# Sample-attention tail of a decoder layer: block choice moved ahead of the value compression

## The chip, the cores and the metric

The kernel runs as one program on one core of a Trainium2 chip (trn2). The metric is the device time of one execution in microseconds (us), the median of several runs. [...]

## What is computed

One decoder layer serves a prompt of 512 rows and 8 sample rows with the same weights. After the input projection, each sample row attends in three ways (native sparse attention) and to a memory; the outputs are normed, projected, and followed by a mixture of 32 experts. The part that the change touches is the attention of the 8 sample rows, over caches of 1024 past rows:

```python
def compress_blocks(rows, pe, w1, w2):      # blocks of 32 rows, every 16 rows
    ...
    return jax.nn.gelu(flat @ w1) @ w2      # once for keys (kc), once for values (vc)

def nsa_core(q, q_pos, gates, kc, vc, kc_end, ks_blk, vs_blk, kw, vw, kw_pos):
    ...
    p_c = masked_softmax(s_c, ...)          # s_c = q . kc, compressed branch
    o_c = p_c @ vc
    imp = sum of p_c over the heads of a group, then over the 4 compressed blocks of a selected block
    top_s, idx = lax.top_k(imp + forced, 16)    # block choice
    o_s = masked_softmax(q . k_sel) @ v_sel     # selected branch
    o_w = masked_softmax(q . kw) @ vw           # window branch
    return gates[..., 0:1] * o_c + gates[..., 1:2] * o_s + gates[..., 2:3] * o_w
```

So the compressed keys are needed for the block choice, and the compressed values only for `o_c`. With 16 of 17 blocks chosen, the choice is one block of the past to leave out.

## The kernel before

The program is written by engine: for each stage, a function for TensorE (`tensor`), VectorE (`vector`), ScalarE (`scalar`), GpSimd (`gpsimd`) and the DMA queue of SyncE (`sync`) writes that engine's instructions in the order in which they will run. Semaphores tie them together: an engine stops at a `wait_ge`, and all that is behind it in its list stops with it. `Chain.then` (L172) counts VectorE's steps in the semaphore `steps_d`; `marks[...]` are counts at named steps on which other engines wait.

`project_and_stream` (L1028) runs two stages as one block: `project` and `stream`. `stream` (L494) reads the caches sequence by sequence, turns them (transposes on TensorE), and forms the scores of the 8 sample rows as each sequence passes. Compression goes in three groups of three sequences, `j` = 0, 1, 2. For a group, `compress(j, q, taps)` (L880) accumulates 16 taps (matmuls of 128x378) for keys (`q` = 0) or values (`q` = 1) in PSUM bank 6 or 7; `gelu(j, q)` (L586) is five VectorE steps with one ScalarE `tanh` (L810) between the fourth and the fifth; `blocks_k` (L921) and `blocks_v` (L928) apply the second weight; `keep_k` and `keep_v` (L600, L604) copy the result to SBUF.

The change lies in the tail of `stream`, after the last sequence, where only group 2 is left. The order of each engine's list there is:

- TensorE (L958 to L1022): the key taps of group 2; the last sequence's scores; ten value taps; `blocks_k(2)`; six value taps; the compressed scores (L966, "cs"); `blocks_v(2)`; the sum of importances (L971, waits for the mark `pc`); the transposes of memory, window and compressed probabilities (L975 to L980, wait for `wp` and `cg`); a matmul with zeros that clears the output bank (L985); a wait for the turned probabilities in SBUF (`pT_ready` 1); a second clearing matmul (L992); value products of the window branch (L994, L997), of the compressed branch (L999) and of the memory (L1002); the transposes of the selected probabilities (L1005, L1006, wait for `sp`); a wait (`pT_ready` 2); value products of the selected branch (L1009, L1012); a wait (`oT_ready`); the gathering of all outputs into one row per sequence (L1021).
- VectorE (L656 to L713): `gelu(2, 0)`; peaks of the memory scores and window scores; `keep_k(2)`; `gelu(2, 1)`; `keep_v(2)`; softmax weights of memory and window (mark `wp`); the peak of the compressed scores (mark `cmax`), their weights (`pc`), their gate (`cg`); the block choice (L684 to L693); the peak of the selected scores (`smax`); four copies of turned probabilities from PSUM (L697 to L700); weights of the selected branch (`sp`); two copies (L706, L707); copies of the outputs (L709, L710) and of the gathered rows (L712, L713).
- ScalarE (L826 to L840): `tanh(2, 0)`, the exponentials of memory, window, `tanh(2, 1)`, the exponentials of the compressed and the selected scores.

GpSimd and SyncE have finished their lists of this stage by then. The block ends with a barrier of all engines (L1058, `close`, L194), and all that follows (`attend` for the prompt, the output projection, the experts with their weight streaming) is issued behind it; the first instruction behind it on SyncE is L1194.

## Time and profile before

| | us |
|---|---|
| median of 3 runs | 1080.23 (1079.83 to 1081.94) |
| span of the profiled execution, first to last instruction | 1077.6 |
| lies around the span, by the median | 2.6 |
| tail of `stream`: first value tap of group 2 to the end of the last copy | 289.89 to 333.92 |
| first DMA issue behind the barrier | 335.05 |

The profile gives no other time of the profiled execution than its span; the 2.6 us are the difference to the median of the runs. Over the whole span TensorE is busy 85%, VectorE 30%, ScalarE 18%, GpSimd 10%. Times in the rows below are us from the start of the span, durations us unless marked ns. One float32 matmul shows as two records, so "x20" are ten taps.

### The profile page before, as it was taken

To read this page: it belongs to the slowest core of one execution; us is meant where nothing else is said; L and a number is where in the kernel's file an instruction comes from. 1 tells how busy PE (TensorE), PEld (TensorE's weight loads), DVE (VectorE), ACT (ScalarE), POOL (GpSimd) and SP (SyncE) were. 2 spreads that over 40 slices of the span, in tenths; PEclk is the share of its full clock that TensorE was granted. 3 is DMA by queue.
4 is the path that set the end of the run, shared out by engine and by line. 5 is a ranking of instruction groups with operands and counts; after the bars stand their busy time and mean duration, and the time that the engine had idled before them with its cause. 6 is when DMAs were issued, how large, how long until landed. Compare 5 with 4: busy or idle time off the path is not lost.

```text
span 1077.6 us, 13517 instructions
## 1 busy us (share of the span) xinstructions
PE 913.1 (85%) x5419; PEld 496.5 (46%) x5419; DVE 324.4 (30%) x697; ACT 193.2 (18%) x462; POOL 112.9 (10%) x131
## 2 busy tenths in 40 slices
PE   3899969999967798799999899979887777787874
PEld 2455535555536454444556555535443334344441
DVE  3333242323244368864625111111110111111110
ACT  1111122112102456563100010000000000000000
POOL 0000114121000000000000012111110111110111
PEclk9999988999979768989998999999999999999998
DMA  9754017495405200003748999999999999999992
GB/s 387 319 174 125 15 55 182 109 222 121 134 1 183 102 1 1 1 1 149 296 184 319 360 415 417 408 417 418 407 419 416 416 413 410 409 419 414 412 418 72
DMA packets 66055, 273.14 MB, mean 253 GB/s; under 512 B 11760, under 2 KB 27951, under 8 KB 40575
## 3 DMA queue, kind: packets, MB, share of 16 engines
q1 hardware_dynamic: 52215, 255.22, 60.7%
q0 software_dynamic: 7376, 12.85, 4.4%
q10 hardware_dynamic: 6400, 4.20, 1.7%
q8 instruction: 44, 0.72, 0.3%
q14 instruction: 20, 0.16, 0.0%
HBM read 265.68 MB, written 19.10 MB: 264 GB/s over the span
## 4 chain that ended last, share of the span: by engine, by line
PE 27%; DMA 23%; SPq 8%; DVE 6%; ACT 3%; issue 1%; POOL 0%; DVEq 0%; POOLq 0%
DMA room<-in_w_up 13%; PE ps L2149 8%; SPq L2011 6%; PE ps L1721 5%; DMA w_a<-in_w_gate 5%; PE ps L2176 4%; DMA w_b<-in_w_up 3%; SPq L2015 2%; ACT w_a L1561 2%; DVE room L1426 2%; PE ps L1254 1%; PE ps L1272 1%; PE ps L1304 1%; PE ps L2163 1%; DMA xg<-hn_dram,pairs 1%
## 5 line engine op out<-in xcount | busy, mean ns | idle before, releaser
L2149 PE MATMUL ps<-room 128*64 128x256 f32 x800 | 98.1, 393 | 32.2 <-DMA room<-in_w_up 19.5
L2149 PEld LDWEIGHTS ps<-room 128*64 128x64 f32 x800 | 56.5, 140 | 70.2 <-DMA room<-in_w_up 28.7
L2149 PE MATMUL ps<-w_a,room 128*64 128x256 f32 x576 | 69.3, 390 | 17.2 <-DMA w_a<-in_w_up 9.3
L2149 PE MATMUL ps<-w_b,room 128*64 128x256 f32 x576 | 67.8, 383 | 17.8 <-DMA w_b<-in_w_up 9.5
L445 PE MATMUL ps<-w_b,room 128*128 128x454 f32 (+1 forms) x240 | 81.6, 551 | 0.7 <-ACT room L418 0.7
L2065 POOL DMA_INDIRECT out_y<-room,halves x32 | 50.1, 1566 | 286.4 <-ACT room L2329 286.4
L2329 ACT ACTIVATE room<-ps,slot_w 128x512 f32<-128x512 f32 x32 | 22.0, 687 | 281.0 <-PE ps L2176 281.0
L894 PE MATMUL ps<-room,w_a 128*128 128x378 f32 x192 | 62.0, 482 | 0.0
L2149 PEld LDWEIGHTS ps<-w_a,room 128*64 128x64 f32 x576 | 41.1, 139 | 42.7 <-DMA w_a<-in_w_up 13.9
L2149 PEld LDWEIGHTS ps<-w_b,room 128*64 128x64 f32 x576 | 40.2, 137 | 42.7 <-DMA w_b<-in_w_up 14.6
L2240 DVE SCALAR_TENSOR_TENSOR room<-room,ps 128x256 f32<-128x256 f32 x32 | 13.5, 422 | 152.6 <-ACT room L2323 152.6
L1721 PE MATMUL ps<-w_b,room 128*128 128x512 f32 x128 | 57.7, 608 | 0.0
L445 PEld LDWEIGHTS ps<-w_b,room 128*128 128x128 f32 (+1 forms) x240 | 38.1, 173 | 40.1 <-issue 40.1
L2242 DVE TENSOR_TENSOR room<-room,ps 128x256 f32<-128x256 f32 x32 | 13.5, 422 | 138.3 <-PE ps L2149 138.3
L2176 PE MATMUL ps<-room,consts 128*64 128x512 f32 x208 | 47.6, 598 | 0.5 <-DVE consts L2246 0.5
L1561 ACT ACTIVATE w_a<-ps,room 128x256 f32<-128x256 f32 (+3 forms) x80 | 40.4, 516 | 41.7 <-DVE room L1426 41.6
L894 PEld LDWEIGHTS ps<-room,w_a 128*128 128x128 f32 x192 | 36.1, 190 | 23.2
L2246 DVE COPY consts<-ps 128x256 f32<-128x256 f32 x32 | 13.6, 425 | 106.5 <-PE ps L2133 106.5
L2323 ACT ACTIVATE room<-ps 128x256 f32<-128x256 f32 x32 | 12.3, 384 | 169.5 <-PE ps L2149 169.5
L1272 PE MATMUL ps<-consts,w_a 128*128 128x128 f32 x160 | 25.2, 302 | 16.7 <-DVE xg L1511 5.7
L2019 POOL DMA_INDIRECT xg<-hn_dram,pairs x16 | 17.0, 1062 | 212.2 <-PE ps L2163 126.3
L584 DVE COPY room<-ps 128x512 f32<-128x512 f32 x33 | 22.8, 692 | 54.3 <-PE ps L855 41.8
(356 smaller groups left out, 1203.6 us busy)
## 6 DMA issues: line engine op xcount, KB each, us to landing
room<-in_w_down SPq DMA_DIRECT2D x26, 1024.0 KB, 28.8
room<-in_w_gate SPq DMA_DIRECT2D x25, 1024.0 KB, 28.4
room<-in_w_up SPq DMA_DIRECT2D x25, 1024.0 KB, 28.3
w_a<-in_w_gate SPq DMA_DIRECT2D x18, 1024.0 KB, 27.8
w_a<-in_w_up SPq DMA_DIRECT2D x18, 1024.0 KB, 28.5
w_a<-in_w_down SPq DMA_DIRECT2D x18, 1024.0 KB, 28.0
w_b<-in_w_gate SPq DMA_DIRECT2D x18, 1024.0 KB, 27.6
w_b<-in_w_up SPq DMA_DIRECT2D x18, 1024.0 KB, 28.3
```

The lines of the kernel that those rows point to most:

```text
L445: ins = nc.tensor.matmul(in_psum(t, a), xT[:, t % 2, k, 0:r], rhs, start=(k == 0), stop=(k == KD - 1))
L584: nc.vector.tensor_copy(dst, src).then_inc(out_d, 1)
L894: ins = nc.tensor.matmul(ps[:, 6 + q, 0:NG3], w1[:, q, l, :], XT[q][:, :, :, l % 8, l // 8:l // 8 + NC_S].rearrange("p s g m -> p (s g) m" ...
L1272: ins = nc.tensor.transpose(ps[:, 4 + j, 128 * c:128 * c + 128], probS[:, int(kind == "win"), j, w * c + 128 * k:w * c + 128 * k + 128], i ...
L1426: low = nc.vector.tensor_reduce(top.rearrange("p (j n) -> p j n", j=2), sc, AX.X, ALU.min)
L1561: ins = nc.scalar.activation(pr[:, i // n, i % n, :], sc[:, i // n, i % n, :], ACT.Exp, bias=stt[:, u % 6, 0, i:i + 1], scale=-1.0, accum_ ...
L1721: ins = nc.tensor.matmul(ps[0:r, b + a, :], m[:, k, :], w_out[:, k, 512 * a:512 * a + 512], start=(k == 0), stop=(k == KD - 1))
L2011: sp.dma_start(self.gate_or_up(u, j), src[:, 4 * j:4 * j + 4, :]).then_inc(self.unit_in[j][u % RING], 16)
L2065: pool.indirect_dma_start(out=rows, out_offset=bass.IndirectOffsetOnAxis(ap=self.halves[:, n:n + 1].bitcast(U32), axis=0), in_=yb[:, slot, ...
L2149: ins = nc.tensor.matmul(ps[h * CAP:h * CAP + CAP, bank, 0:FH], xT[:, n // 2 % 2, k, CAP * slot:CAP * slot + CAP], w[k // 4][:, k % 4, h * ...
L2176: ins = nc.tensor.matmul(ps[a * CAP:a * CAP + CAP, 6 + n % 2, :], hT[:, j, h * CAP:h * CAP + CAP], wd[h][:, j, 512 * a:512 * a + 512], sta ...
L2329: nc.scalar.activation(yb[:, n % 2, :], ps[0:2 * CAP, 6 + n % 2, :], ACT.Copy, scale=self.slot_w[:, n:n + 1]).then_inc(y_copied, 1)
```

## The change

The diff reorders the tail of `stream`, engine by engine.

- TensorE: `blocks_k(2)` comes after four value taps instead of ten, cs after six, L971 after ten, and the last six value taps follow it. `blocks_v(2)` moves to the middle of the selected branch's products, and the compressed branch's products, which need it, to the end. The clearing matmuls stand together, ahead of the transposes of the selected probabilities, which stand ahead of all value products. The outputs gather in bank 2 (`win0`) instead of bank 7 (`cmp_`). The memory rows are gathered ahead of the others.
- VectorE: `gelu(2, 1)` and `keep_v(2)` move from ahead of the softmaxes to behind the last of them; the weights of the window branch move behind the block choice; six copies of turned probabilities and two of outputs leave its list.
- ScalarE: it takes the six copies of turned probabilities, the copy `om` of the memory outputs and the last copy into `o_s`. `tanh(2, 1)` stands behind the copies of the turned probabilities.
- Two semaphores are new, `om_in_psum` and `om_ready`.

```diff
@@ vector @@
+            keep_k(2)
             peak(2, 64, swb[:, 1:513], "wmax")
-            keep_k(2)
-            gelu(2, 1)
-            keep_v(2)
-
-            dve.wait_ge(es, 1)
-            weights(1, 32, smb[:, :], None, None)
-            dve.wait_ge(gate_in, 16 * NB)
-            dve.wait_ge(es, 2)
-            weights(2, 64, swb[:, 1:513], g64[:, 2:3], None)
-            ch.then(nc.vector.tensor_scalar(dgn[:, 1, :], self.c(C_ID, 64, 64), swb[:, 512:513], None, ALU.mult))
-            marks["wp"] = ch.n
             dve.wait_ge(cs_in_psum, 1)
             ch.then(nc.vector.tensor_copy(scb[:, 0:NC_S], misc[0:64, 0:NC_S]))
             peak(0, 64, scb[:, 0:NC_S], "cmax")
+            dve.wait_ge(es, 1)
+            weights(1, 32, smb[:, :], None, None)
             dve.wait_ge(es, 3)
             weights(0, 64, scb[:, 0:NC_S], None, "pc")
 
+            dve.wait_ge(gate_in, 16 * NB)
             dve.wait_ge(imp_in_psum, 1)
...
             peak(3, 64, ssb[:, 0:1025], "smax")
-            dve.wait_ge(pT_in_psum, 1)
-            nc.vector.tensor_copy(late[:, 1568:1824], ps[:, 5, 0:256])
...
+            dve.wait_ge(es, 2)
+            weights(2, 64, swb[:, 1:513], g64[:, 2:3], None)
+            ch.then(nc.vector.tensor_scalar(dgn[:, 1, :], self.c(C_ID, 64, 64), swb[:, 512:513], None, ALU.mult))
+            marks["wp"] = ch.n
             dve.wait_ge(es, 4)
             weights(3, 64, ssb[:, 0:1025], g64[:, 1:2], None)
...
             marks["sp"] = ch.n
-            dve.wait_ge(pT_in_psum, 2)
-            nc.vector.tensor_copy(late[:, 1888:2400], ps[:, 4, :])
-            nc.vector.tensor_copy(nw[:, 0, :], hid[0:NB, 256:320]).then_inc(pT_ready, 1)
+            gelu(2, 1)
+            keep_v(2)
             dve.wait_ge(o_in_psum, 4)
-            nc.vector.tensor_copy(oa, cmp_[:, 0:256])
-            nc.vector.tensor_copy(om, ps[:, 0, :]).then_inc(oT_ready, 1)
+            nc.vector.tensor_copy(oa, win0[:, 0:256]).then_inc(oT_ready, 1)
             dve.wait_ge(os_in_psum, 1)
             nc.vector.tensor_copy(self.o_s[:, 0:512], ps[0:NB, 4, :])
-            nc.vector.tensor_copy(self.o_s[:, 512:768], ps[0:NB, 5, 0:256])
@@ scalar @@
-            tanh(2, 1)
-
             act.wait_ge(steps_d, marks["cmax"])
...
+            act.wait_ge(pT_in_psum, 1)
+            nc.scalar.copy(late[:, 1568:1824], ps[:, 5, 0:256])
+            nc.scalar.copy(pTc[0:NC_S, :], ps[0:NC_S, 5, 256:320])
+            nc.scalar.copy(late[:, 1824:1888], ps[:, 5, 448:512])
+            nc.scalar.copy(nw[:, 1, :], ps[0:NB, 5, 384:448]).then_inc(pT_ready, 1)
+            act.wait_ge(pT_in_psum, 2)
+            nc.scalar.copy(late[:, 1888:2400], ps[:, 4, :])
+            nc.scalar.copy(nw[:, 0, :], hid[0:NB, 256:320]).then_inc(pT_ready, 1)
+            tanh(2, 1)
+            act.wait_ge(om_in_psum, 4)
+            nc.scalar.copy(om, ps[:, 0, :]).then_inc(om_ready, 1)
+            act.wait_ge(os_in_psum, 1)
+            nc.scalar.copy(self.o_s[:, 512:768], ps[0:NB, 5, 0:256])
@@ tensor @@
-            compress(2, 1, range(10))
+
+            compress(2, 1, range(4))
             blocks_k(2)
-            compress(2, 1, range(10, 16))
+            compress(2, 1, range(4, 6))
             pe.wait_ge(kc_ready, 3)
...
             ins.then_inc(cs_in_psum, 1)
-            blocks_v(2)
-
+            compress(2, 1, range(6, 10))
             pe.wait_ge(steps_d, marks["pc"])
             nc.tensor.matmul(hid[0:64, 0:64], self.c(C_RG, 64, 64), scb[:, :], start=True, stop=True).then_inc(imp_in_psum, 1)
+            compress(2, 1, range(10, 16))
...
-            pe.wait_ge(steps_d, marks["cg"])
             nc.tensor.transpose(ps[0:NC_S, 5, 256:320], scb[:, 0:NC_S], ident(64)).then_inc(pT_in_psum, 1)
...
-            pe.wait_ge(vc_ready, 3)
-            nc.tensor.matmul(cmp_, zb2[0:1, 0:128], zb2[0:1, :], start=True, stop=False, skip_group_check=True)
+            nc.tensor.matmul(win0, zb2[0:1, 0:128], zb2[0:1, :], start=True, stop=False, skip_group_check=True)
+            nc.tensor.matmul(ps[:, 0, :], zb2[0:1, 0:128], zb2[0:1, :], start=True, stop=False, skip_group_check=True)
+            pe.wait_ge(steps_d, marks["sp"])
+            for j in range(8):
+                nc.tensor.transpose(ps[:, 4, 64 * j:64 * j + 64], ssb[:, 128 * j:128 * j + 128], ident(64))
+            nc.tensor.matmul(hid[0:NB, 256:320], self.c(C_S8, NB, 64), dgn[:, 0, :], start=True, stop=True).then_inc(pT_in_psum, 1)
...
             pe.wait_ge(pT_ready, 1)
...
-            for b in range(NB):
-                nc.tensor.matmul(o(b), pTc[0:NC_S, heads(b)], vc[0:NC_S, place[b], :], **add)
...
             pe.wait_ge(pT_ready, 2)
...
-            for j in range(8):
+            for j in range(4):
                 for b in range(NB):
...
+                    nc.tensor.matmul(o(b), pTs[:, j, heads(b)], Vs[:, b, j // 2, j % 2, :], **add)
+            blocks_v(2)
+            for j in range(4, 8):
+                for b in range(NB):
+                    nc.tensor.matmul(o(b), pTs[:, j, heads(b)], Vs[:, b, j // 2, j % 2, :], **add)
+            pe.wait_ge(vc_ready, 3)
+            for b in range(NB):
+                ins = nc.tensor.matmul(o(b), pTc[0:NC_S, heads(b)], vc[0:NC_S, place[b], :], **add)
...
-            pe.wait_ge(oT_ready, 1)
-            for n, (src, bank, wide) in enumerate(((oa, 4, 128), (om, 5, 256))):
+            for n, (src, bank, wide) in ((1, (om, 5, 256)), (0, (oa, 4, 128))):
+                if n == 1:
+                    pe.wait_ge(om_ready, 1)
+                else:
+                    pe.wait_ge(oT_ready, 1)
```

## Rows read from the trace of the kernel before

**Rows 1.** The page: span of the profiled execution.
```profile
span 1077.6 us, 13517 instructions
```
**Rows 2.** Timeline, TensorE, 289 to 334: start, duration, instruction, [idle before, its releaser].
```profile
289.89 6.62 PE L894 MATMUL ps<-room,w_a 128*128 128x378 f32 x20
296.35 0.80 PE L925 MATMUL ps<-room 128*128 128x189 f32 x4
296.99 3.97 PE L894 MATMUL ps<-room,w_a 128*128 128x378 f32 x12
300.89 1.14 PE L966 MATMUL ps<-spare,room 128*64 128x63 f32 x16
304.37 0.90 PE L931 MATMUL ps<-room 128*63 128x64 f32 x12 [2.34 <-DVE room L598]
309.09 0.47 PE L971 MATMUL ps<-room,consts 64*64 64x64 f32 x2 [3.81 <-DVE room L639]
...
310.76 0.36 PE L980 MATMUL ps<-consts,room 64*63 64x64 f32 x1
...
314.87 0.58 PE L992 MATMUL ps<-w_a 1*128 1x512 bf16 x1 [3.21 <-DVE w_a L700]
...
316.34 3.60 PE L997 MATMUL ps<-w_b,w_a 128*8 128x128 f32 x64
319.88 1.04 PE L999 MATMUL ps<-spare,w_a 63*8 63x128 f32 x16
320.84 1.91 PE L1002 MATMUL ps<-w_a 128*4 128x256 f32 x32
322.69 0.71 PE L1005 MATMUL ps<-consts,w_a 64*128 64x64 f32 x8
...
324.57 0.62 PE L1009 MATMUL ps<-room,w_a 8*8 8x128 f32 x16 [0.97 <-DVE w_a L707]
325.12 3.68 PE L1012 MATMUL ps<-w_b,w_a 128*8 128x128 f32 x128
330.02 2.85 PE L1021 MATMUL ps<-w_a,consts 128*8 128x64 f32 x48 [1.22 <-DVE w_a L710]
```
**Rows 3.** Timeline, VectorE, ScalarE and SyncE's queue, 301 to 336.
```profile
301.00 0.61 DVE L593 TENSOR_SCALAR room<-ps,room 128x378 f32<-128x378 f32 x1 [3.39 <-PE ps L894]
...
306.34 0.15 DVE L637 RECIPROCAL room<-room 64x1 f32<-64x1 f32 x1
...
307.38 0.22 DVE L676 COPY room<-ps 64x63 f32<-64x63 f32 x1
...
309.67 0.24 DVE L682 TENSOR_SCALAR room<-room 64x63 f32<-64x63 f32 x1 [0.64 <-PE ps L971]
...
313.92 1.15 ACT L839 ACTIVATE w_a<-w_a,room 64x1025 f32<-64x1025 f32 x1 [5.42 <-DVE room L633]
...
316.23 0.25 DVE L703 TENSOR_SCALAR w_a<-consts,w_a 64x64 f32<-64x64 f32 x1
...
333.52 0.40 DVE L713 COPY spare<-ps 8x256 f32<-8x256 f32 x1
...
335.05 0.37 SPq L1194 DMA_DIRECT2D w_b<-in_bands  x1
```
**Rows 4.** Windows: stretch, its us, busy us of each engine, PEclk, DMA share, GB/s.
```profile
302.10:304.30 2.20, 0.00 (x0) 0.00 (x0) 1.55 (x4) 0.52 (x1) 0.00 (x0) 1.00 0.00 0
305.30:309.00 3.70, 0.00 (x0) 0.00 (x0) 2.83 (x11) 0.44 (x2) 0.00 (x0) 0.75 0.00 0
307.20:320.70 13.50, 8.41 (x109) 4.71 (x109) 7.07 (x24) 1.68 (x4) 0.00 (x0) 0.50 0.01 1
335.00:478.00 143.00, 116.36 (x670) 67.33 (x670) 93.96 (x202) 82.08 (x253) 4.70 (x4) 0.81 0.14 54
```
**Rows 5.** Groups of ScalarE by line and shape, whole span: busy us, mean ns, idle.
```profile
L805 ACT COPY room<-ps 128x512 f32<-128x512 f32 x33 | 19.3, 584 | 62.5 <-PE ps L855 39.5 <-PE ps L859 14.4 <-PE ps L863 6.1
...
L1585 ACT COPY room<-ps 128x256 f32<-128x256 f32 x4 | 1.5, 386 | 0.0
```

More of the change, by code:

```diff
@@ L529, in stream @@
         gate_out, gate_in, gclamp, gexp, gsig = (S(n) for n in ("gate_out", "gate_in", "gclamp", "gexp", "gsig"))
+        om_in_psum, om_ready = S("om_in_psum"), S("om_ready")
         scored, cs_in_psum, ec, pc, imp_in_psum, es, ps_ready, pT_in_psum, pT_ready, o_in_psum, oT_ready, os_in_psum = (S(n) for n in (
@@ L695, in vector @@
             peak(3, 64, ssb[:, 0:1025], "smax")
-            dve.wait_ge(pT_in_psum, 1)
-            nc.vector.tensor_copy(late[:, 1568:1824], ps[:, 5, 0:256])
-            nc.vector.tensor_copy(pTc[0:NC_S, :], ps[0:NC_S, 5, 256:320])
-            nc.vector.tensor_copy(late[:, 1824:1888], ps[:, 5, 448:512])
-            nc.vector.tensor_copy(nw[:, 1, :], ps[0:NB, 5, 384:448]).then_inc(pT_ready, 1)
+            dve.wait_ge(es, 2)
+            weights(2, 64, swb[:, 1:513], g64[:, 2:3], None)
+            ch.then(nc.vector.tensor_scalar(dgn[:, 1, :], self.c(C_ID, 64, 64), swb[:, 512:513], None, ALU.mult))
+            marks["wp"] = ch.n
             dve.wait_ge(es, 4)
@@ L991, in tensor @@
             pe.wait_ge(pT_ready, 1)
-            nc.tensor.matmul(ps[:, 0, :], zb2[0:1, 0:128], zb2[0:1, :], start=True, stop=False, skip_group_check=True)
             for b in range(NB):
@@ L997, in tensor @@
                     nc.tensor.matmul(o(b), pTw[:, j, heads(b)], Vw[:, b, j, :], **add)
-            for b in range(NB):
-                nc.tensor.matmul(o(b), pTc[0:NC_S, heads(b)], vc[0:NC_S, place[b], :], **add)
             for j in range(2):
                 for b in range(NB):
-                    nc.tensor.matmul(ps[at(b, 4), 0, 256 * (b // 4):256 * (b // 4) + 256], pTm[:, j, 4 * b:4 * b + 4], Vm[b // 4][:, b % 4, j, :], **add)
-            pe.wait_ge(steps_d, marks["sp"])
-            for j in range(8):
-                nc.tensor.transpose(ps[:, 4, 64 * j:64 * j + 64], ssb[:, 128 * j:128 * j + 128], ident(64))
-            nc.tensor.matmul(hid[0:NB, 256:320], self.c(C_S8, NB, 64), dgn[:, 0, :], start=True, stop=True).then_inc(pT_in_psum, 1)
+                    ins = nc.tensor.matmul(ps[at(b, 4), 0, 256 * (b // 4):256 * (b // 4) + 256], pTm[:, j, 4 * b:4 * b + 4], Vm[b // 4][:, b % 4, j, :], **add)
+                    if j == 1 and b >= NB - 4:
+                        ins.then_inc(om_in_psum, 1)
             pe.wait_ge(pT_ready, 2)
@@ L1009, in tensor @@
                 nc.tensor.matmul(o(b), nw[:, 0, heads(b)], z[0:NB, smp, V0 + 128:V0 + 256], **add)
-            for j in range(8):
+            for j in range(4):
                 for b in range(NB):
-                    ins = nc.tensor.matmul(o(b), pTs[:, j, heads(b)], Vs[:, b, j // 2, j % 2, :], **add)
-                    if j == 7 and b >= NB - 4:
-                        ins.then_inc(o_in_psum, 1)
-            pe.wait_ge(oT_ready, 1)
-            for n, (src, bank, wide) in enumerate(((oa, 4, 128), (om, 5, 256))):
+                    nc.tensor.matmul(o(b), pTs[:, j, heads(b)], Vs[:, b, j // 2, j % 2, :], **add)
[6 more added lines that the diff above has]
+                ins = nc.tensor.matmul(o(b), pTc[0:NC_S, heads(b)], vc[0:NC_S, place[b], :], **add)
+                if b >= NB - 4:
+                    ins.then_inc(o_in_psum, 1)
+            for n, (src, bank, wide) in ((1, (om, 5, 256)), (0, (oa, 4, 128))):
[3 more added lines that the diff above has]
+                    pe.wait_ge(oT_ready, 1)
                 for c in range(H if n == 0 else MH):
```

2 lines of the change are left out of this document (1 added, 1 removed).

## The prediction, made before the changed kernel ran

> **What bounds the kernel now.** I read the page first, then the timeline of TensorE in the tail of `stream`, then that of the other engines, and last the granted clock by windows. The profiled span is 1077.6 us [rows 1]; the runs' median of 1080.23 lies 2.6 above it, and I carry these 2.6 over unchanged, so every us taken from the span is taken from the median. In the tail, TensorE's list is worked through from 289.89 to 332.87 (330.02 and 2.85 of L1021) and five times it stands still for another engine: 2.34, 3.81, 3.21, 0.97 and 1.22, together 11.55 us [rows 2]. In each of these waits a single chain of small VectorE and ScalarE steps runs and nothing else does: from 302.10 to 304.30 TensorE, GpSimd and the DMAs are at 0.00 [rows 4]. So the tail is one serial chain that changes engines, and TensorE's work lies in it one piece at a time instead of beside the others. The clock makes it worse: it is granted at 1.00 through the first wait, falls in the second (mean 0.75 from 305.30 to 309.00) and is 0.50 from 307.20 to 320.70 [rows 4]. What stands behind the barrier begins with SyncE's L1194 at 335.05 [rows 3], 2.18 after TensorE's end, and every engine's work from there on is issued behind it. So I expect all of it to move as one block.
>
> **The change, step by step.** I lay the new lists against the clock of the trace, from 289.89, before which nothing changes. TensorE's pieces keep their durations: a value tap is 0.66 (6.62 for ten), `blocks_k` 0.80, cs 1.14 [rows 2]. The new order puts four taps (2.65), `blocks_k` (0.80), two taps (1.32), cs (1.14) and four taps (2.65) ahead of L971, which starts at 298.45 instead of 309.09.
>
> Two handovers lie inside. `keep_k` copies 189 columns while two taps run (1.32); a copy of 256 columns took VectorE 0.40 [rows 3], so it is hidden with some 0.8 to spare. The mark `pc` took from L676's start to L971's start, 307.38 to 309.09, 1.71 [rows 2, 3]; counted from cs's end at 295.8 it comes at 297.5, with 0.9 to spare behind the four taps. The memory weights, now between the peak and these weights, lie beside ScalarE's exponential. The wait for the gates moves ahead of the choice and costs nothing: no DMA is under way in this part [rows 4].
>
> From L971 the chain goes through VectorE as before. L682 starts 0.58 behind L971 (309.09 to 309.67; that was at the low clock, I keep it), the exponential of the selected scores 4.25 after that (313.92), and the mark `sp` 2.56 after its start (L703's end, 316.48) [rows 2, 3]. That gives 299.03, 303.28 and `sp` at 305.84. The window weights, 1.04 (306.34 to 307.38) [rows 3], go into the 1.15 in which VectorE waits for the exponential [rows 3]; `wp` comes at 304.3. What this moves: six taps, 3.97, now run beside the choice, and TensorE ends them at 302.9 (L971 0.47 before them) [rows 2]. So the new wait is 302.9 to 304.3, 1.4. Everything on TensorE is queued behind it, and ScalarE's copies wait for the transposes that come next.
>
> The transposes of the first group took 1.56 (309.56, the end of L971, to 311.12, the end of L980) [rows 2] at 0.50 of the clock. At the full clock their bounds are half of it, 0.78, and 1.56; I take 1.1, since part of such short pieces is filling and draining: 305.4. A clearing matmul was 0.58 at the low clock (L992) [rows 2]; two at the full clock lie between nothing, where they only fill the wait for `sp`, and 1.16; I take 0.6: 306.0, so `sp` is there. The selected transposes and their last row took 0.91 (L1005's start at 322.69 to L1009's at 324.57, less its wait of 0.97) [rows 2]: 306.9.
>
> The copies for `pT_ready` 1 run on ScalarE meanwhile. The trace of before has no narrow one; the nearest row is 386 ns for 128x256 [rows 5], which the first has; the other three are narrower, so all four take 0.39 to 1.54. I take 1.1: ready at 306.6, at worst 307.05. So the products start at 306.9; in the kernel before, the first started between L992 and L997. The copies for `pT_ready` 2 are 0.58 and at most 0.39 [rows 5], ready at 307.9, and are wanted at 311.3: hidden, with 3.4 to spare.
>
> The products at the full clock: the window's own row like L1009, 0.62; its four parts half of L1012's 3.68, 1.84 (they took 3.60 at the low clock); the memory 1.91; the selected own row 0.62; half the selected parts 1.84; `blocks_v` 0.90; the other half 1.84; the compressed branch, of L1009's count and near shape, 0.62 instead of 1.04 [rows 2]. That is 10.19, to 317.1. `gelu(2, 1)` took from L593's start to L931's start, 301.00 to 304.37, 3.37 [rows 2, 3]; begun at `sp` it is ready at 309.2, and `blocks_v` wants it at 313.7: 4.5 to spare. `keep_v` has a half of the selected parts, 1.84, as its cover. The gathering is 2.85 for 48 records [rows 2]; the memory's 16 come first, 0.95. They cover the copy `oa`: the wait of 1.22 there was for two copies in a row, the larger of which (`om`) now lies under 5 us of products. So the gathering ends at 319.9 instead of 332.87, 12.9 earlier.
>
> Two corrections. The last copy (0.40) [rows 3] goes to ScalarE and runs beside the other: 0 to 0.4 saved, I take 0.3. And the pieces overlap in the pipeline: the first four of rows 2 sum to 12.53 and took 12.14 (289.89 to 302.03) [rows 2], so my sum is too long by 0.4. Together 12.9 + 0.3 + 0.4 = **13.6 us**, so 1080.23 − 13.6 = **1066.6**. A second account as a bound: of the 11.55 of waits 1.4 remain, and of the 8.0 us of work at the low clock (309.09 to 311.12, 314.87 to 320.84) [rows 2, 4] at most half goes: 10.15 + 4.0 + 0.3 = 14.5. The unknown copies and transposes, at their bad ends together, take some 1.5 from the 13.6. With the spread of the runs, about 1 to either side, the forecast's own range is 1064.5 to 1069.
>
> **The rivals.**
>
> *The clock stays low in the products.* The level fell after a stretch with 3.81 us of waiting that followed only 0.90 of work, and it held through 2.34 of waiting that followed steady taps [rows 2, 4]. The new order has steady taps, a wait of 1.4, then thin transposes. I think it holds. If it falls there and stays down as long as before, 13.5 us [rows 4], the work from 304.3 goes at half speed: at most 6.75 lost, 1073.4; a shorter stay gives some 1070. [...]
>
> *ScalarE's queue makes `blocks_v` late.* `tanh(2, 1)` now stands behind six copies and two waits on TensorE; a late transpose holds it up, VectorE's last gelu step waits with it, `keep_v` and `oa` are queued behind that, and TensorE waits in the middle of the products. It decides from 4.5 us of delay on, and costs what goes beyond: with 6.5 us of delay 2 are lost, 1068.6. Nothing in the rows is of that size.
>
> *The gain is given back.* If the work behind the barrier waited for something that doesn't move with it, the time would be 1080. Against it: the DMAs and SyncE's queue are empty ahead of 335.05 [rows 3, 4].
>
> *Slower.* The prompt's attention behind the barrier alternates between the two levels: its mean is 0.81 over 143 us [rows 4], so some 54 us (0.19 of 143, twice) are spent at the low one. If entering it from another rhythm, or at another phase, lets it stay low for longer, each us at half speed loses at most half a us. It turns slower than before by over 0.2% from some 32 us more of it on (16 us to lose: 13.6 and 2.2), that is 86 of the 143 or a mean under 0.70: 1082.4 and more. I see no reason for such a shift, only that this stretch is sensitive.
>
> **How the numbers follow.** Chances: the forecast 0.79, the low clock 0.09, ScalarE's queue 0.03, given back 0.04, slower 0.05. Differences under 0.2% (2.2 us) can't be told from no change here. Faster: 0.79 + 0.09 + 0.03 = 0.91; same 0.04; slower 0.05. The range goes from 1064.0, the second account with half the runs' spread more, to 1073.4, the low clock's price; it leaves out the last two cases, 0.09.
>
> **What would show it.** In the changed kernel's timeline L971's successor should start near 298.4, the exponential of the selected scores near 303.2, the first product near 306.9, `blocks_v` without a wait near 313.7, and SyncE's first issue behind the barrier near 321.5; TensorE should have one wait of over 1 us, at `wp`. The clock should be 1.00 from 289 to 321. The tail's gain and the span's gain should be equal within 1 us. I am wrong if the products show twice these durations, if a wait stands ahead of `blocks_v` or of the gathering, or if the stretch behind the barrier is longer than before.

## The result and the profile after

The changed kernel takes 1065.76 us (median of 4 runs, 1061.26 to 1066.78) against 1080.95 of the kernel before, run beside it (1079.83 to 1081.94): a ratio of 0.9876, 95% interval 0.9837 to 0.9915. The forecast was 1066.6, range 1064.0 to 1073.4. Two later comparisons, each with the kernel before beside it, gave 0.9896 (0.9872 to 0.9921; 1066.70 against 1076.48) and 0.9898 (0.9858 to 0.9938; 1065.48 against 1079.21). In us the three gains are 15.2, 9.8 and 13.7; the forecast was 13.6.

The page gives the span, to be set beside [rows 1].

```profile
span 1063.1 us, 13517 instructions
```

The timeline of TensorE in the tail answers to [rows 2]: start, duration, instruction, and in brackets the idle time before it. Lines are those of the changed kernel; L974 is the old L971, L979 opens the window's transposes, L986 is the first clearing matmul, L990 opens the selected transposes, L999, L1002 and L1005 are the old L994, L997 and L1002, L934 is `blocks_v`, L1032 the gathering.

```profile
291.15 2.81 PE L897 MATMUL ps<-room,w_a 128*128 128x378 f32 x8
...
299.61 0.33 PE L974 MATMUL ps<-room,consts 64*64 64x64 f32 x2
...
305.39 0.30 PE L979 MATMUL ps<-consts,w_a 32*128 32x32 f32 x2 [1.44 <-DVE w_a L693]
...
306.41 0.39 PE L986 MATMUL ps<-w_a 1*128 1x512 bf16 x1
...
307.00 0.71 PE L990 MATMUL ps<-consts,w_a 64*128 64x64 f32 x8
...
307.85 0.62 PE L999 MATMUL ps<-room,w_a 8*8 8x128 f32 x16
...
308.39 2.91 PE L1002 MATMUL ps<-w_b,w_a 128*8 128x128 f32 x64
...
311.06 2.67 PE L1005 MATMUL ps<-w_a 128*4 128x256 f32 x32
...
316.07 0.90 PE L934 MATMUL ps<-room 128*63 128x64 f32 x12
...
319.32 2.85 PE L1032 MATMUL ps<-w_a,consts 128*8 128x64 f32 x48
```

The same timeline for VectorE, ScalarE and SyncE's queue answers to [rows 3].

```profile
304.32 1.15 ACT L828 ACTIVATE w_a<-w_a,room 64x1025 f32<-64x1025 f32 x1 [6.15 <-DVE room L634]
...
306.52 0.37 ACT L832 COPY w_a<-ps 128x256 f32<-128x256 f32 x1 [0.96 <-PE ps L983]
...
306.70 0.25 DVE L697 TENSOR_SCALAR w_a<-consts,w_a 64x64 f32<-64x64 f32 x1
...
306.99 0.20 ACT L835 COPY w_a<-ps 8x64 f32<-8x64 f32 x1
...
309.74 0.55 DVE L599 SCALAR_TENSOR_TENSOR room<-spare,room 128x378 f32<-128x378 f32 x1 [0.58 <-ACT spare L803]
...
322.20 0.68 DVE L704 COPY spare<-ps 8x512 f32<-8x512 f32 x1 [2.25 <-PE ps L1032]
...
324.03 0.37 SPq L1205 DMA_DIRECT2D w_b<-in_bands  x1
```

By windows (stretch, its us, busy us of TensorE, its weight loads, VectorE, ScalarE, GpSimd, then TensorE's granted clock, DMA share, GB/s), against [rows 4]. The profile gives the granted clock as a share of full speed; in all fourteen traces each of its records is 0.50 or 1.00, which are the two levels of the prediction, and a value between is the mean of a stretch with both.

```profile
305.40:307.80 2.40, 2.40 (x21) 1.50 (x21) 1.99 (x5) 0.83 (x6) 0.00 (x0) 1.00 0.00 0
...
309.30:312.50 3.20, 3.20 (x56) 2.09 (x50) 0.55 (x1) 0.41 (x1) 0.00 (x0) 0.50 0.00 0
```
```profile
321.00:464.00 143.00, 110.22 (x700) 65.25 (x698) 95.55 (x205) 82.28 (x254) 4.69 (x4) 0.87 0.15 54
```

Read together: of five waits on TensorE one is left, 1.44 us ahead of L979. The tail, from the first value tap to the end of the last copy, takes 31.73 us (291.15 to 322.88) instead of 44.03 (289.89 to 333.92). That is 12.30, and the span is 14.5 shorter. The rest lies outside the tail: it began 1.26 later, and the stretch from SyncE's first issue behind the barrier to the end took 739.1 us instead of 742.6, with a mean clock of 0.87 instead of 0.81 in its first 143 (the window shown begins 3 us ahead of it, with the same mean). And in the middle of the products the clock fell to 0.50: L1002 took 2.91, L1005 2.67 (1.93 and 1.91 in filler, at 1.00). Three questions were left for experiments: which parts of the change brought the 12.30, why the clock fell although TensorE no longer waited long, and whether the 3.5 us behind the barrier belong to the change.

### The profile page after: what moved, and what is told of

The parts are those of the page before. It is cut to its first block, busy times and chain, and to the rows that moved or that the text cites. A ratio compares the mean times of both kernels' runs of the same rounds, so it can differ in the third digit from the quotient of the medians.

```text
span 1063.1 us, 13517 instructions
## 1 busy us (share of the span) xinstructions
PE 903.8 (85%) x5419; PEld 493.8 (46%) x5419; DVE 321.4 (30%) x689; ACT 195.3 (18%) x470; POOL 112.8 (11%) x131
## 4 chain that ended last, share of the span: by engine, by line
PE 24%; DMA 23%; SPq 12%; DVE 6%; ACT 3%; issue 1%; POOL 0%; DVEq 0%; POOLq 0%; ACTq 0%
DMA room<-in_w_up 11%; SPq L2022 8%; PE ps L2160 6%; PE ps L1732 5%; SPq L2026 3%; PE ps L2187 3%; DMA w_b<-in_w_up 3%; DMA w_a<-in_w_gate 3%; DMA w_b<-in_w_gate 3%; DMA room<-in_w_gate 3%; DVE room L1437 2%; ACT w_a L1572 2%; PE ps L1283 1%; PE ps L1265 1%; DMA xg<-hn_dram,pairs 1%
## 5 line engine op out<-in xcount | busy, mean ns | idle before, releaser
L2257 DVE COPY consts<-ps 128x256 f32<-128x256 f32 x32 | 13.6, 425 | 106.5 <-PE ps L2144 106.5
```

## Experiments

All kernels start from the changed one and compute the whole layer; the filled forms add matmuls whose sum nobody reads, as their edit says. Each is compared with the kernel before, run beside it. "Low" is the time at 0.50 of the clock by the granted-clock records.

| kernel | median us, ratio to before (95%) | tail us | low in the tail | behind the barrier us | low in its first 143 |
|---|---|---|---|---|---|
| before | – | 44.03 | 13.7 | 742.6 | 54.6 |
| changed, 1st trace | 1065.76, 0.9876 (0.9837 to 0.9915) | 31.73 | 3.4 | 739.1 | 37.5 |
| after_again | 1066.70, 0.9896 (0.9872 to 0.9921) | 32.99 | 6.8 | 741.1 | 58.0 |
| after_third | 1065.48, 0.9898 (0.9858 to 0.9938) | 31.73 | 3.4 | 738.9 | 51.2 |
| taps_first | 1071.17, 0.9939 (0.9915 to 0.9964) | 37.97 | 10.2 | 741.4 | 58.0 |
| choice_alone | 1070.94, 0.9933 (0.9909 to 0.9958) | 39.33 | 10.2 | 744.1 | 62.8 |
| copies_on_vector | 1066.78, 0.9905 (0.9867 to 0.9943) | 31.82 | 3.4 | 742.3 | 58.0 |
| values_early | 1067.88, 0.9879 (0.9846 to 0.9912) | 35.43 | 10.2 | 738.3 | 37.5 |
| outputs_on_vector | 1067.09, 0.9887 (0.9865 to 0.9909) | 31.68 | 0 | 741.5 | 51.2 |
| filler | 1063.49, 0.9846 (0.9824 to 0.9868) | 30.06 | 0 | 740.7 | 44.4 |
| filler_again | 1063.69, 0.9865 (0.9828 to 0.9902) | 31.67 | 3.4 | 744.5 | 63.4 |
| copies_filler | 1065.19, 0.9890 (0.9854 to 0.9926) | 31.76 | 3.4 | 744.7 | 63.3 |
| window_early | 1062.90, 0.9836 (0.9814 to 0.9858) | 28.80 | 0 | 743.8 | 62.8 |
| window_early_again | 1061.28, 0.9859 (0.9824 to 0.9895) | 28.79 | 0 | 737.8 | 37.5 |

The four columns on the right come from one profiled execution each, the medians from four to six runs.

By their medians only taps_first and choice_alone are clearly slower than the changed kernel: none of their runs (1068.5 us and more) comes down to those of after_again beside them (1064.20 to 1067.65). For copies_on_vector, values_early and outputs_on_vector the whole time shows no difference: their ratios, 0.9905, 0.9879 and 0.9887, lie among or within 0.001 of the changed kernel's three. What is said of these three rests on the waits and the tail of one trace each.

### taps_first

```diff
-            compress(2, 1, range(6, 10))
+            compress(2, 1, range(6, 16))
             pe.wait_ge(steps_d, marks["pc"])
...
-            compress(2, 1, range(10, 16))
```

> The changed kernel with one thing undone: the last six value taps stand ahead of the sum of importances again, so that the block choice waits for them. The tail (first value tap of group 2 to the end of its last copy) was 44.03 us before and 31.73 us in the changed kernel. Theory A, the choice is the chain that sets the tail and the taps are hidden beside it: the tail grows by the taps' 4.0 us to 35.7, and by up to 3 us more if TensorE's longer wait (some 5.5 us) lets the clock fall. Theory B, what counts is that VectorE was relieved by ScalarE: the tail stays at 31.7.

The wait at the window's transposes, in TensorE's timeline, and the clock behind it by windows:

```profile
307.83 0.42 PE L978 MATMUL ps<-consts,w_a 32*128 32x32 f32 x2 [5.46 <-DVE w_a L693]
```
```profile
307.90:317.20 9.30, 9.30 (x113) 5.47 (x117) 3.84 (x8) 1.87 (x9) 0.00 (x0) 0.50 0.01 2
```

The wait grew from 1.44 to 5.46, by 4.02, which is what six taps cost; the low clock takes the other 2.2, tail 37.97. The clock fell within this wait, at 307.11. The taps beside the choice are worth their whole length, and theory B is out: this kernel kept all of ScalarE's copies.

### copies_on_vector

The block moved is the six copies with their two waits, from ScalarE's list to VectorE's.

```diff
             marks["sp"] = ch.n
+            dve.wait_ge(pT_in_psum, 1)
+            nc.vector.tensor_copy(late[:, 1568:1824], ps[:, 5, 0:256])
...
+            nc.vector.tensor_copy(nw[:, 0, :], hid[0:NB, 256:320]).then_inc(pT_ready, 1)
             gelu(2, 1)
...
-            act.wait_ge(pT_in_psum, 1)
-            nc.scalar.copy(late[:, 1568:1824], ps[:, 5, 0:256])
...
-            nc.scalar.copy(nw[:, 0, :], hid[0:NB, 256:320]).then_inc(pT_ready, 1)
```

> The changed kernel with one thing undone: the six copies of turned probabilities are VectorE's again, behind the mark sp and ahead of the value gelu. Theory A: VectorE is free for them when they come; the first four end about when the first product can start, and the gelu has 5.8 us to spare and loses 1.9; the tail stays within 0.4 of 31.73. Theory B: the copies and the gelu stand in line on VectorE again, the tail grows by 2 us or more.

Its tail is 31.82 against 31.73 with as much low clock; in its timeline the first product follows the selected transposes without a wait:

```profile
305.02 0.28 PE L991 MATMUL ps<-w_a,consts 64*8 64x64 f32 x2
305.32 0.62 PE L999 MATMUL ps<-room,w_a 8*8 8x128 f32 x16
```

So moving the six copies to ScalarE brought nothing that shows. VectorE is free for them once the value gelu stands behind.

### values_early

```diff
+            blocks_v(2)
             pe.wait_ge(v_in, 16 * 2 * NB)
...
                     nc.tensor.matmul(o(b), pTw[:, j, heads(b)], Vw[:, b, j, :], **add)
+            pe.wait_ge(vc_ready, 3)
+            for b in range(NB):
+                nc.tensor.matmul(o(b), pTc[0:NC_S, heads(b)], vc[0:NC_S, place[b], :], **add)
...
-            blocks_v(2)
...
-            pe.wait_ge(vc_ready, 3)
-            for b in range(NB):
-                ins = nc.tensor.matmul(o(b), pTc[0:NC_S, heads(b)], vc[0:NC_S, place[b], :], **add)
```

> The changed kernel with one thing undone: the second value weight stands ahead of all products and the compressed products behind the window's, as before the change. Theory A: TensorE waits some 2.5 us for the value gelu (ready 19.1 us behind the first tap, the first product at 16.7), so the tail is 34 us and, with a longer fall of the clock, up to 36. Theory B, the order of the products is of no account since TensorE's sum is the same: 31.7.

```profile
310.56 1.54 PE L934 MATMUL ps<-room 128*63 128x64 f32 x12 [1.77 <-DVE room L599]
```

In its timeline `blocks_v` waits 1.77 for the last gelu step. The rest of the 3.7 us is clock: 10.2 us at 0.50 in place of 3.4, which also stretches `blocks_v` from 0.90 to 1.54 and the transposes ahead of it, so that the wait is shorter than the 2.5 expected. Theory A holds for the tail: the late place of the compressed branch is worth the wait. The median, 0.9879 of before, doesn't show it.

### outputs_on_vector

```diff
-            nc.vector.tensor_copy(oa, win0[:, 0:256]).then_inc(oT_ready, 1)
+            nc.vector.tensor_copy(oa, win0[:, 0:256])
+            nc.vector.tensor_copy(om, ps[:, 0, :]).then_inc(oT_ready, 1)
...
+            nc.vector.tensor_copy(self.o_s[:, 512:768], ps[0:NB, 5, 0:256])
...
-            act.wait_ge(om_in_psum, 4)
-            nc.scalar.copy(om, ps[:, 0, :]).then_inc(om_ready, 1)
-            act.wait_ge(os_in_psum, 1)
-            nc.scalar.copy(self.o_s[:, 512:768], ps[0:NB, 5, 0:256])
...
-            for n, (src, bank, wide) in ((1, (om, 5, 256)), (0, (oa, 4, 128))):
...
+            pe.wait_ge(oT_ready, 1)
+            for n, (src, bank, wide) in enumerate(((oa, 4, 128), (om, 5, 256))):
```

> The changed kernel with one thing undone: both output copies on VectorE behind the last product, all gathering behind them, and both last copies on VectorE. Theory A: the wait of 1.22 us ahead of the gathering and 0.3 us of the last copy come back, tail 33.2 us at the clock of the first trace (3.4 us at 0.50), 1.3 more at that of the second. Theory B: the copies are hidden anyway, 31.7.

```profile
318.75 2.85 PE L1025 MATMUL ps<-w_a,consts 128*8 128x64 f32 x48 [1.22 <-DVE w_a L703]
```
```profile
291.00:321.00 30.00, 27.33 (x401) 18.92 (x401) 14.86 (x42) 4.96 (x15) 0.00 (x0) 1.00 0.01 2
```

The wait of 1.22 is back. The tail of 31.68 hides this at first sight: the clock held in this trace, 1.00 throughout. Beside the filled form's 30.06, which held too, it is 1.62 longer: 1.22 of wait and some 0.4, for the most part the last copy, which stands behind another one again. The expected 33.2 failed only in the clock.

### choice_alone

The edits of copies_on_vector, values_early and outputs_on_vector together.

```diff
+            dve.wait_ge(pT_in_psum, 1)
...
+            nc.vector.tensor_copy(om, ps[:, 0, :]).then_inc(oT_ready, 1)
...
+            blocks_v(2)
             pe.wait_ge(v_in, 16 * 2 * NB)
...
+            pe.wait_ge(oT_ready, 1)
+            for n, (src, bank, wide) in enumerate(((oa, 4, 128), (om, 5, 256))):
```

> The early choice alone: the changed kernel with the copies of turned probabilities back on VectorE, the outputs copied and gathered as before, and the second value weight and the compressed products ahead of the selected branch. Theory A: the outputs cost 1.5 us (a wait of 1.2 and a copy of 0.3), and TensorE waits some 4.3 us for the value gelu, which now starts behind six copies and is wanted at the start of the products; the tail is 37.5, so the early choice alone brings 6.5 of the 12.3. Theory B: the relief of VectorE is undone, the tail is back at 42 or more.

```profile
310.52 1.54 PE L932 MATMUL ps<-room 128*63 128x64 f32 x12 [4.13 <-DVE room L599]
```
```profile
325.06 2.85 PE L1025 MATMUL ps<-w_a,consts 128*8 128x64 f32 x48 [1.22 <-DVE w_a L711]
```

The waits are as expected, 4.13 and 1.22, and the tail is 39.33, 1.8 over the forecast, with 10.2 us of low clock. So the early choice without these three parts brings 4.7 of the 12.30. The parts don't add up singly: the copies cost nothing by themselves, but with `blocks_v` early they delay the gelu that TensorE then waits for. `blocks_v` starts 20.89 us behind the first tap (310.52 less 289.63) against 19.51 in values_early (310.56 less 291.05), 1.38 later; the rest of the difference between the waits, 4.13 and 1.77, is that in values_early the low clock stretched the transposes ahead of them.

### after_again and after_third

Both are the changed kernel.

> The changed kernel once more, for a second trace. In the first one the stretch from the first issue behind the barrier to the end was 739.1 us, 3.5 shorter than before, with a granted clock of 0.87 instead of 0.81 in its first 143 us, and the clock fell to 0.50 for 3.4 us in the middle of the value products. Theory A, these are chance of the clock and no effect of the change: the stretch is anywhere from 738 to 744 us, and goes with the clock's mean; the tail is 30 where the clock holds and 31.7 where it falls. Theory C, the change itself makes the prompt's attention faster: 739 again, within 0.5.

> The changed kernel a third time, beside its filled and reordered forms on the same chip. Of four traces with its order up to the products (after, after_again, copies_on_vector, outputs_on_vector) three showed the clock at 0.50 for 3.4 to 6.8 us in the tail and one did not. Theory A, the 1.44 us wait lets the clock fall, in most runs: it falls here with chances 3 in 4, tail 31.7 to 33; where it holds, 30.0. Behind the barrier 738 to 744 us.

The window's transposes and products in after_again, where the low stretch was longer and came earlier, and the clock by windows:

```profile
303.64 0.30 PE L979 MATMUL ps<-consts,w_a 32*128 32x32 f32 x2 [1.45 <-DVE w_a L693]
...
305.73 1.11 PE L990 MATMUL ps<-consts,w_a 64*128 64x64 f32 x8
...
308.04 3.47 PE L1002 MATMUL ps<-w_b,w_a 128*8 128x128 f32 x64
```
```profile
303.64:304.42 0.78, 0.78 (x8) 0.61 (x8) 0.47 (x2) 0.17 (x2) 0.00 (x0) 1.00 0.00 0
304.42:311.25 6.83, 6.83 (x95) 4.11 (x97) 3.36 (x7) 1.77 (x7) 0.00 (x0) 0.50 0.01 2
```

The clock fell in all three traces of this kernel, for 3.4, 6.8 and 3.4 us, but not at one place: here 0.78 us into the transposes, right behind the wait of 1.45; in the first trace at 309.18 and in after_third at 309.06, each 1.3 us into the products. The tail of 32.99 is over both values of Theory A, as the low stretch was twice as long. Behind the barrier it took 739.1, 741.1 and 738.9. The expected link between that time and the low clock holds roughly and not to the us: 51.2 us low went with 738.9 in after_third and 741.5 in outputs_on_vector. Theory C, a repeat within 0.5, fails on the 741.1. The question returns with window_early.

### filler, filler_again and copies_filler

```diff
             compress(2, 1, range(10, 16))
+            for l in range(2):
+                nc.tensor.matmul(ps[:, 2, 0:NG3], w1[:, 1, l, :], XT[1][:, :, :, l % 8, l // 8:l // 8 + NC_S].rearrange("p s g m -> p (s g) m"), start=True, stop=True)
```

copies_filler has the edit of copies_on_vector as well.

> The changed kernel with two more matmuls of a value tap's shape, whose sum nobody reads, in TensorE's wait of 1.44 us ahead of the window's transposes; they take some 1.3 us, so that nothing comes later. In three traces of that order (after, after_again, copies_on_vector) the clock fell to 0.50 for 3.4 to 6.8 us behind this wait. Theory A, the wait is what lets the clock fall: it stays at 1.00 through the tail, which takes 30.0 us. Theory B, the narrow transposes and clearing matmuls behind the wait do it: the clock falls as before, 31.7 to 33.0 us.

> The filled form once more. Its first trace held 1.00 through the tail (30.06 us), but so did one of four traces without the filler, so one trace decides little. Theory A, the wait lets the clock fall: 1.00 again, tail 30.1, and its median time 1 to 2 us below that of after_third. Theory B, it was luck: the clock falls with the same chance of 3 in 4, tail 31.7 to 33, and the medians agree within 0.7 us.

> The filled form with the six copies of turned probabilities on VectorE. Theory A on the copies (they are free there as well) and on the wait: tail 30.1 with the clock at 1.00. If the copies do cost something, which a fallen clock may have hidden in copies_on_vector (31.82), the tail is 30.5 or more. If the filler does nothing for the clock: 31.8.

The wait is gone (TensorE's timeline of filler; L977 is the filler, L981 opens the window's transposes):

```profile
303.32 1.43 PE L977 MATMUL ps<-room,w_a 128*128 128x378 f32 x4
304.93 0.30 PE L981 MATMUL ps<-consts,w_a 32*128 32x32 f32 x2 [0.18 <-DVE w_a L693]
```

In filler the clock held, tail 30.06. In the other two it fell all the same. Windows of filler_again: the taps and the filler, the transposes with the clearing matmuls, the products:

```profile
290.60:304.60 14.00, 14.00 (x60) 8.42 (x58) 9.31 (x31) 2.69 (x7) 0.00 (x0) 1.00 0.00 0
304.85:307.30 2.45, 2.45 (x22) 1.50 (x22) 2.04 (x5) 0.84 (x6) 0.00 (x0) 1.00 0.00 0
307.50:310.80 3.30, 3.30 (x68) 2.15 (x64) 1.59 (x4) 1.10 (x3) 0.00 (x0) 0.50 0.02 5
```

And of copies_filler, the transposes and the products:

```profile
306.12:308.60 2.48, 2.48 (x21) 1.51 (x21) 2.02 (x7) 0.17 (x2) 0.00 (x0) 1.00 0.00 0
308.90:312.20 3.30, 3.30 (x68) 2.16 (x60) 2.61 (x7) 0.52 (x1) 0.00 (x0) 0.50 0.02 5
```

My theory, that the wait lets the clock fall, doesn't hold as it stands: the wait isn't needed. TensorE has no wait over 0.18 us in the 17 us before, is busy in every bit of the transposes' stretch, and the clock goes to 0.50 within 0.3 us of its end (at 307.41 and 308.88). With the wait it fell in 4 of 5 traces (the three of the changed kernel and copies_on_vector, not outputs_on_vector), without it in 2 of 3. What all eight share is the stretch of about 2.5 us of transposes, matmuls of 8 columns and clearing matmuls of one row, called the narrow stretch below. That it is the cause isn't shown: in after_again the clock fell before most of it had run and right behind the wait, and in two of the eight traces it held. In values_early the fall came inside this stretch too, in taps_first and choice_alone inside longer waits; these three say nothing of the fillers' question.

The medians point the other way from the tails: filler_again's is 1.8 us below after_third's in the same comparison (1063.69 and 1065.48), as Theory A had it, though their profiled tails are 31.67 and 31.73. The single runs overlap widely (1058.98 to 1069.95 and 1062.40 to 1070.57), so this settles nothing. The copies on VectorE cost nothing with the wait filled either: 31.76 against filler_again's 31.67.

### window_early and window_early_again

The window's weights move into VectorE's wait for the importances, their transposes between the thirteenth and the fourteenth tap, the four copies of them on ScalarE ahead of the selected exponential, and the selected transposes from ahead of the window's products to between these and the memory's. The edit's core:

```diff
@@ vector @@
             dve.wait_ge(gate_in, 16 * NB)
+            dve.wait_ge(es, 2)
+            weights(2, 64, swb[:, 1:513], g64[:, 2:3], None)
+            ch.then(nc.vector.tensor_scalar(dgn[:, 1, :], self.c(C_ID, 64, 64), swb[:, 512:513], None, ALU.mult))
+            marks["wp"] = ch.n
             dve.wait_ge(imp_in_psum, 1)
...
             ch.then(nc.vector.tensor_copy(ssb[:, 1024:1025], misc[0:64, 64:65]))
+            marks["sel"] = ch.n
@@ scalar @@
-            act.wait_ge(steps_d, marks["smax"])
...
             act.wait_ge(pT_in_psum, 1)
...
+            act.wait_ge(steps_d, marks["smax"])
...
@@ tensor @@
-            compress(2, 1, range(10, 16))
...
-            pe.wait_ge(steps_d, marks["wp"])
+            compress(2, 1, range(10, 13))
+            pe.wait_ge(steps_d, marks["cg"])
...
+            compress(2, 1, range(13, 16))
...
+            pe.wait_ge(steps_d, marks["sel"])
...
-            pe.wait_ge(steps_d, marks["sp"])
...
+            pe.wait_ge(steps_d, marks["sp"])
...
```

> The changed kernel with the window's weights moved into VectorE's wait for the importances (1.35 us idle, 1.0 needed), their transposes among the last six value taps, the copies of them ahead of the exponential of the selected scores, and the window's products ahead of the selected transposes. TensorE should have no wait of over 0.3 us left in the tail: the wait of 1.44 at wp and some 0.5 around sp go. If the clock holds, its fall of 3.4 us (1.7 us lost) goes too: tail 28 us, against 31.73 and 32.99. If the clock falls all the same: 30. If the early window weights hold up the choice (the rival), the exponential of the selected scores starts later than 14.9 us behind the first tap and up to 1 us is lost: 31.

> The reordered form once more. Theory A: the clock holds as in its first trace, tail 28.8, and the median lies 3 us below after_third (1.44 of the wait, 1.5 of the clock) and 1.3 below filler_again. If the clock's fall was absent by luck: 28.8 plus 1.3 to 1.9.

VectorE in window_early: the window's last step ends as the importances come, so the choice (L680 on) loses nothing, and the exponential of the selected scores starts 13.1 us behind the first tap (304.52 less 291.38).

```profile
299.75 0.25 DVE L677 TENSOR_SCALAR w_a<-consts,w_a 64x64 f32<-64x64 f32 x1
...
300.27 0.24 DVE L680 TENSOR_SCALAR room<-room 64x63 f32<-64x63 f32 x1 [0.28 <-PE ps L975]
...
304.52 1.15 ACT L834 ACTIVATE w_a<-w_a,room 64x1025 f32<-64x1025 f32 x1 [0.52 <-DVE room L634]
```

TensorE in window_early, the clearing matmuls and `blocks_v`:

```profile
305.33 0.38 PE L988 MATMUL ps<-w_a 1*128 1x512 bf16 x1
...
313.37 0.90 PE L935 MATMUL ps<-room 128*63 128x64 f32 x12
```

Windows of window_early (the tail; the first 143 us behind the barrier; the rest), then of window_early_again:

```profile
291.40:319.40 28.00, 28.00 (x408) 19.16 (x407) 14.28 (x41) 5.46 (x16) 0.00 (x0) 1.00 0.01 2
321.32:464.32 143.00, 116.83 (x665) 68.29 (x666) 93.40 (x202) 80.74 (x251) 4.70 (x4) 0.78 0.15 54
464.32:1065.10 600.78, 511.55 (x3361) 271.02 (x3360) 120.81 (x270) 57.59 (x113) 68.91 (x51) 0.98 0.89 359
```
```profile
290.80:318.80 28.00, 28.00 (x408) 19.15 (x407) 14.26 (x41) 5.45 (x16) 0.00 (x0) 1.00 0.01 2
320.71:463.71 143.00, 112.11 (x702) 67.50 (x702) 97.39 (x212) 84.36 (x259) 4.69 (x4) 0.87 0.15 54
463.71:1058.50 594.79, 507.96 (x3324) 268.92 (x3322) 116.18 (x260) 53.68 (x103) 68.85 (x51) 0.97 0.90 363
```

Three things are read here. TensorE is busy 28.00 of 28.00 us in the tail: no wait is left in it, and a shorter tail now needs less work on TensorE. The whole tail is 28.80, 0.8 over what was expected. The clock held in both traces, in which taps and the window's products stand between the pieces of the narrow stretch; if the chance of holding were still that of the eight traces, 2 in 8, two in a row would come 1 time in 16, so this speaks for the narrow stretch as the cause and doesn't prove it: this form has no wait either. And narrow work alone doesn't always bring the fall: from 305.33 to 313.37 TensorE has only clearing matmuls, transposes and products of 8 or 4 columns, 8.0 us of them, at 1.00. What lets the clock fall in this tail stays open. And one and the same kernel takes 743.8 and 737.8 us behind the barrier, with a clock of 0.78 and 0.87: the 3.5 us by which the changed kernel's first trace was shorter there lie within this chance. Theory A of after_again holds on that point, and its Theory C is out.

Its median is 4.2 us below after_third in the same comparison (1061.28 and 1065.48) and 2.4 below filler_again, where 3 and 1.3 were expected; the tails account for 2.94, and the chance behind the barrier for the rest as far as these runs tell. This version beats both kernels: 16.6 and 17.9 us below the kernel before.

## Why the prediction was right, step by step

Right as a whole, and for the mechanism named, though that the number came so close is luck in part: the tail was one chain through all engines, and the choice's steps with TensorE's taps laid beside them set the gain. In us behind the first value tap:

| step | forecast | changed kernel | filler, clock held |
|---|---|---|---|
| importances (old L971) | 8.6 | 8.46 | 8.46 |
| exponential of the selected scores | 13.4 | 13.17 | |
| TensorE's wait for the window weights | 1.4 | 1.44 | 0.18 |
| first product | 17.0 | 16.70 | 16.70 |
| value gelu ready | 19.3 | 19.14 | |
| `blocks_v` | 23.8 | 24.92 | 23.25 |
| gathering starts | 27.2 | 28.17 | 26.50 |
| first issue behind the barrier | 31.6 | 32.88 | 31.21 |

*The chain up to the first product* held within 0.3 us. Of the unknown costs, the transposes took 1.10 (L979 at 305.39 to the end of L983 at 306.49) where I took 1.1; that is 0.71 of their 1.56 at 0.50 [rows 2], so not half; that filling and draining make the difference was my estimate, and no run shows it. The clearing matmuls took 0.59 (306.41 to 307.00) for 0.6, the four copies on ScalarE 0.67 (306.52 to 307.19) for 1.1, below the middle of my bounds, 0.39 to 1.54. None of the copies was late, so this error cost nothing. I had written that the trace of before has no narrow copy on ScalarE; it has two of 128x64, at 196 and 213 ns, by which four in a row make some 1.0, and in the changed kernel the four overlap (0.37, 0.20, 0.21 and 0.20, together 0.98, in 0.67):

```profile
L1805 ACT COPY room<-ps 128x64 f32<-128x64 f32 x1 | 0.2, 213 | 13.0 <-PE ps L1740 13.0
L404 ACT COPY room<-ps 128x64 f32<-128x64 f32 x1 | 0.2, 196 | 0.0
```

*The clock* is the step that failed. I expected 1.00 from 289 to 321 and priced the products at that; they ran partly at 0.50, and L1002 and L1005 took 5.58 together, where half of L1012 with L1002 of [rows 2] gave 3.75: 1.83 too little. Where the clock held they took 3.84 (1.93 and 1.91 in filler), so the pieces were priced rightly and the clock wasn't. The rival "the clock stays low in the products" had this mechanism, and a price for a shorter stay, some 1070; for its cause it named the wait and the thin transposes behind it and left open which. The fillers show that the wait isn't needed (0.18 us of it left, and a fall in two of three), and no run shows more. The row that the rival argued from was also read loosely: in the kernel before, the clock didn't fall behind 3.81 us of waiting but inside it, since a mean of 0.75 over 305.30 to 309.00 [rows 4] is half of that stretch at 0.50. TensorE's busy time, as the profile counts it, doesn't settle it: in filler_again it is busy for 2.45 of 2.45 us (304.85 to 307.30), and the clock fell behind them, at 307.41; in filler it is just as busy there, and the clock held. Nor does the order of work: with the narrow stretch in one piece and the products right behind it the clock fell in six traces and held in two.

*The second account*, 14.5 as a bound on the tail's gain, is met where the clock held: 44.03 less 30.06 is 13.97, of which the filled wait is no part, since the window's transposes start 14.24 us behind the first tap with the filler (304.93 less 290.69) and without (305.39 less 291.15). The bound itself left out one low-clock piece, the clearing matmul L985 (0.60 from 311.06), and would be some 0.3 higher with it.

*The other rivals.* ScalarE's queue: `blocks_v` had 5.8 us to spare (gelu ready at 310.29, wanted at 316.07) where I worked out 4.5, so `tanh` behind the copies cost nothing. The gain was not given back: the block behind the barrier moved as a whole. "Slower" from the prompt's attention: that stretch does vary, over 6.9 us in fourteen traces (737.8 to 744.7, with 37.5 and 63.3 us of low clock in its first 143), but far from the 16 that this rival needed.

*That the tail's gain and the span's agree within 1 us* was wrong: 12.30 and 14.5. The forecast of 1066.6 comes within 0.9 of the median with errors of opposite sign in the profiled run: 1.83 lost in the products and 1.26 by which the tail began later, against 3.5 gained behind the barrier, which the runs show to be chance. That they nearly cancel is luck. Its own range, 1064.5 to 1069, holds all three medians of the changed kernel; a single run is wider (1061.26 to 1070.57 in the three comparisons), which I had put at about 1 to either side. Two slips in the working changed nothing that followed: 305.4 with 1.1 and 1.54 for the copies gives 306.5 and 306.9, where I had 306.6 and 307.05; and 14.5 with half the runs' spread gives a lower end of 1064.7 for the range, where I had 1064.0.

*What each part was worth*, by undoing it, with the clock's share told apart: the six taps beside the choice 4.02 (taps_first); the outputs' order and copies 1.62 (outputs_on_vector against filler, both at the full clock); the late compressed branch a wait of 1.77, at a stretched clock (values_early); the copies on ScalarE alone 0.1 (copies_on_vector). What is left of the 12.30 isn't told apart by edit: no run undid the move of the value gelu alone, and the kernel before had 13.7 us of low clock in its tail where the changed one had 3.4. By sort it can be: TensorE's waits went from 11.55 to 1.44, which is 10.11; from TensorE's end to the end of the last copy it took 0.71 (322.17 to 322.88) instead of 1.05 (332.87 to 333.92), which is 0.34; the 1.85 left over goes, by this subtraction, to work that no longer ran at the low clock.

## What to carry to other kernels

Where a tail runs through several engines, write down for each wait which chain ends it and lay the longest independent work of the waiting engine beside that chain; here six taps, moved a few lines, were worth their full length, 4.02 us. Moving copies to an idle engine brought nothing that shows here (31.73 against 31.82), since the busy one was free when they came due; to know that, the list must be laid out in time. When no engine waits any more, look at TensorE's clock: 3.4 us at 0.50 cost 1.61 of the tail between two traces of the filled form (31.67 against 30.06). Laying wide matmuls between narrow ones went with a clock that held here, at 1.00 through 28.00 us in two traces; it is worth a try and not shown to be the reason.

## What the runs showed of the hardware

TensorE's clock fell here with no idle time in the 2.4 us before it. It went to 0.50 right behind some 2.5 us of transposes, 8-column matmuls and clearing matmuls with TensorE busy throughout and no wait over 0.18 us in the 17 us before (filler_again, copies_filler). Of the eight traces with that stretch in one piece, at most 1.45 us of waiting ahead of it and the value products right behind it, it fell in six, and not at one place: 0.1 and 0.2 us into the products with the wait filled, 1.3 to 1.5 us into them with the wait (after, after_third, copies_on_vector), and 0.78 us into the stretch itself in after_again. Where taps and products stood between its pieces the clock held in two of two (window_early, window_early_again). Some 3.4 us at 0.50 cost 1.3 to 1.7 us here (32.99 against 31.73, for 6.8 and 3.4 low; 31.67 against 30.06; 5.58 against 3.84 in the two product groups).

The time of an unchanged stretch of 740 us varied by 6.9 us between executions. With 37.5 us of low clock in its first 143 it took 738 to 739 (737.8 to 739.1), with 58 and more 741.1 to 744.7; between these the two don't go together.
